# Two activation buffers of a TensorE-bound kernel laid out with 64 bytes between their chunks

## The reference

```
for i in range(2):                                   # first_block
    z = rmsnorm(x, g_mix) @ w_in                     # 2048 -> 4928
    y = concat(mla attention, gated short conv, gated 31-tap conv + layernorm, retention)
    x = x + y @ w_o                                  # 2048 -> 2048
    uf = causal_dwconv(rmsnorm(x, g_ffn) @ w_up)     # 2048 -> 11264, 3 taps
    x = x + (silu(gate) * up) @ w_down               # 5632 -> 2048
    x = x + (p @ w_pe) * sigmoid(rmsnorm(x, g_pe) @ w_pg)
for l in range(2):                                   # second_block
    q, k, v, gates = split(rms_norm(x, norm_g) @ w_in_2)   # 2048 -> 7700
    mixed = concat(forgetting, differential, block and gated linear attention)
    x = x + mixed @ w_out_2
return rms_norm(x, final_norm_g)
```

## Time and profile before

| | |
|---|---|
| median of three runs | 3352.53 us |
| profiled execution, its own time | 3352.41 us |
| its span, first to last instruction | 3350.2 us |
| busy share TensorE matmul / weight load | 99% / 87% |
| busy share VectorE / ScalarE / GpSimd | 78% / 46% / 26% |
| mean granted TensorE clock | 0.998 |
| DMA | 605 MB, 181 GB/s over the span |

### The profile page before, as it was taken

How to read it: one execution, slowest core, us unless ns; L and a number is a source line. 1 busy time by engine, 2 the same in 40 slices (tenths; PEclk the granted TensorE clock), 3 DMA queues, 4 the chain that set the end, 5 groups by cost and what they waited for, 6 DMA issues and landing times. The chain is left out here.

```text
span 3350.2 us, 53769 instructions
## 1 busy us (share of the span) xinstructions
PE 3327.6 (99%) x20366; PEld 2929.1 (87%) x20366; DVE 2617.8 (78%) x3394; ACT 1531.6 (46%) x1642; POOL 864.2 (26%) x633
## 2 busy tenths in 40 slices
PE   9999999999999999999999999999999999999998
PEld 8989888888888989888888888888888888888897
DVE  8897788787786888887887787867867866678865
ACT  5644444343433556544443434335444444445443
POOL 0422432121122423414332121214432004150004
PEclk9999999999999999999999999999999999999999
DMA  6445555555555554455555555555544455544454
GB/s 241 148 163 176 189 188 189 178 202 177 206 174 189 203 182 165 151 176 187 190 188 178 198 180 199 180 190 200 193 164 153 167 173 189 180 164 151 167 185 151
DMA packets 90647, 605.21 MB, mean 181 GB/s; under 512 B 10192, under 2 KB 10352, under 8 KB 29296
## 3 DMA queue, kind: packets, MB, share of 16 engines
q1 hardware_dynamic: 89424, 599.83, 52.0%
q10 hardware_dynamic: 1056, 3.11, 0.2%
HBM read 600.80 MB, written 2.10 MB: 180 GB/s over the span
## 5 line engine op out<-in xcount | busy, mean ns | idle before, releaser
L642 PE MATMUL bank<-H,whi 128*128 128x512 f32 x6496 | 1574.3, 393 | 1.5 <-DVE z L1661 1.5
L1164 ACT ACTIVATE whi<-raw 128x2048 fp32r<-128x2048 f32 (+2 forms) x609 | 1093.6, 1796 | 1044.6 <-DMA raw<-in_slabs_down 259.8
L1630 DVE TENSOR_TENSOR wlo<-raw,whi 128x2048 fp32r<-128x2048 f32 (+2 forms) x609 | 1328.4, 2181 | 243.2 <-ACT whi L1164 233.1
L642 PEld LDWEIGHTS bank<-H,whi 128*128 128x128 f32 x6496 | 1188.7, 188 | 238.6 <-issue 5.9
L653 PEld LDWEIGHTS bank<-H,wlo 128*128 128x128 f32 x6624 | 849.1, 188 | 34.3
L653 PE MATMUL bank<-H,wlo 128*128 128x256 f32 x6624 | 871.1, 281 | 0.0
L511 POOL TENSOR_TENSOR sqtmp<-tmp 128x256 f32<-128x256 f32 x88 | 218.9, 2488 | 867.8 <-DVE tmp L2211 867.8
L642 PE MATMUL bank<-G,whi 128*128 128x512 f32 x1408 | 343.0, 391 | 0.0
L642 PEld LDWEIGHTS bank<-G,whi 128*128 128x128 f32 x1408 | 255.4, 188 | 48.0
L1564 ACT ACTIVATE G<-sqtmp 128x256 f32 (+1 forms) x88 | 36.8, 418 | 404.0 <-POOL sqtmp L511 404.0
L489 POOL TENSOR_TENSOR sqacc<-sqacc,sqtmp 128x256 f32<-128x256 f32 x119 | 199.4, 1676 | 9.4
(11 more groups left out here) (390 smaller groups left out, 2881.4 us busy)
## 6 DMA issues: line engine op xcount, KB each, us to landing
raw<-in_slabs_up SPq DMA_DIRECT2D x176, 1024.0 KB, 4.8
raw<-in_slabs_down SPq DMA_DIRECT2D x128, 704.0 KB, 4.0
raw<-in_slabs_wo SPq DMA_DIRECT2D x32, 1024.0 KB, 4.8
raw<-in_slabs_pg SPq DMA_DIRECT2D x32, 1024.0 KB, 4.9
raw<-in_slabs_gates SPq DMA_DIRECT2D x32, 1024.0 KB, 4.9
raw<-in_slabs_wout SPq DMA_DIRECT2D x32, 1024.0 KB, 4.8
raw<-in_slabs_sc SPq DMA_DIRECT2D x24, 1024.0 KB, 4.8
raw<-in_slabs_fox SPq DMA_DIRECT2D x24, 1024.0 KB, 4.9
```

The costliest lines, as they stand in the source:

```text
L642: pe.matmul(b[0:r.m, :], whi[:, n % RAW, w], r.src[:, k, :], start=at == 0, stop=False)
L1164: act.activation(whi[:, n % RAW, 0:w], raw[:, n % RAW, 0:w], ACT.Copy).then_inc(S("hi_ready"), 1)
L1630: dve.tensor_tensor(wlo[:, n % RAW, 0:w], raw[:, n % RAW, 0:w], whi[:, n % RAW, 0:w].bitcast(F32), ALU.subtract).then_inc(S("lo_ready"), 1)
```

## The change

Chunks of `H` and of `G` no longer lie end to end: each is followed by 16 unused columns (64 bytes), so that the chunk step is 2112 bytes or 33 pieces. Chunk 0 starts at an even piece, chunk 1 at an odd one, and so on in turn; the stream of a wide or narrow row then starts at the other kind of piece from one product to the next. The second group of `G` starts at an odd piece, and alternates too. `whi`, `wlo`, `raw`, `x`, `z`, `y`, `tmp` and `pT_hl` keep the kind of piece that they had; the three unused tensors are made smaller to make room, so these buffers move by some hundred bytes (`raw` by 768, `whi` by 640, `z` by 256). For alternation within every row the `wout` rows (but for the two that open them) now take their chunks in the order 0 to 15. Apart from this every engine has the same instructions in the same order with the same waits.

```
+SPACED = 2 * T + 16
...
-    H = sb("H", [P, DC, 2 * T], F32R)
-    sb("ahead_of_raw", [P, 80])
+    H_spaced = sb("H", [P, DC, SPACED], F32R)
+    H = [H_spaced[:, c, 0:2 * T] for c in range(DC)]
+    sb("ahead_of_raw", [P, 16])
...
-    sb("ahead_of_whi", [P, 48])
+    sb("ahead_of_whi", [P, 16])
...
-    sb("ahead_of_z", [P, 104])
+    sb("ahead_of_z", [P, 8])
...
-    G = ctx.enter_context(nc.sbuf_tensor("G", [P, 2, GC, 2 * T], F32R))
-    ctx.enter_context(nc.sbuf_tensor("rest_of_y", [P, 48 * T - 2 * GC * 2 * T], F32))
+    G = sb("G", [P, 2, GC, SPACED], F32R)
+    sb("rest_of_y", [P, 48 * T - 2 * GC * SPACED])
+
+    def g_chunk(g, pair):
+
+        if isinstance(pair, int):
+            return G[:, g % 2, pair, 0:2 * T]
+        return G[:, g % 2, bass.ds(pair, 1), 0:2 * T].rearrange("p a t -> p (a t)")
...
-            src = G[:, key[2] % 2]
+            src = [g_chunk(key[2], c) for c in range(GC)]
...
-                        k = at if order is None else order[at]
+                        k = at
...
-                            pe.matmul(b[0:r.m, :], whi[:, n % RAW, w], r.src[:, k, :], start=at == 0, stop=False)
+                            pe.matmul(b[0:r.m, :], whi[:, n % RAW, w], r.src[k], start=at == 0, stop=False)
...
-                        last = pe.matmul(b[0:r.m, 0:T], wlo[:, n % RAW, w], r.src[:, k, 0:T], start=False,
+                        last = pe.matmul(b[0:r.m, 0:T], wlo[:, n % RAW, w], r.src[k][:, 0:T], start=False,
...
-                    high, low = (r.src[:, k, o + t * P:o + (t + 1) * P] for o in (0, T))
+                    high, low = (r.src[k][:, o + t * P:o + (t + 1) * P] for o in (0, T))
...
-                act.activation(H[:, c, 0:T], x[:, c, :], ACT.Copy, scale=col(g, l, c)).then_inc(S("h_hi"), 1)
+                act.activation(H[c][:, 0:T], x[:, c, :], ACT.Copy, scale=col(g, l, c)).then_inc(S("h_hi"), 1)
...
-                dve.scalar_tensor_tensor(H[:, c, T:2 * T], x[:, c, :], col(g, l, c), H[:, c, 0:T].bitcast(F32),
+                dve.scalar_tensor_tensor(H[c][:, T:2 * T], x[:, c, :], col(g, l, c), H[c][:, 0:T].bitcast(F32),
```

More of the change, by code:

```diff
@@ L341, in _build @@
     runs, by, h_free = [], {}, {}
-    sources = {"qn": cq, "qr": cq, "kv": cq[:, 4:6, :]}
+    latent = [cq[:, c, :] for c in range(6)]
+    sources = {"qn": latent[0:4], "qr": latent[0:4], "kv": latent[4:6]}
     for key, _, _, kt, m, count, _, _ in slab_table():
@@ L345, in _build @@
         if key[0] == "down":
-            src = G[:, key[2] % 2]
+            src = [g_chunk(key[2], c) for c in range(GC)]
         elif key[0] == "pe":
-            src = pT_hl[:, key[1]]
+            src = [pT_hl[:, key[1], c, :] for c in range(2)]
         loop = key[0] in ("wo", "up", "down", "pg", "wout")
@@ L512, in activations @@
                 pool.wait_ge(S("g_hi"), base + pair + 1)
-                gg = G[:, g % 2, bass.ds(pair, 1), :].rearrange("p a t -> p (a t)")
+                gg = g_chunk(g, pair)
                 pool.tensor_tensor(gg[:, T:2 * T], act_f[:], gg[:, 0:T].bitcast(F32),
@@ L584, in high_first @@
                     w = slice(k * r.m, (k + 1) * r.m)
-                    pe.matmul(b[:, 0:T], whi[:, n % RAW, w], r.src[:, k, 0:T], start=k == chunks[0], stop=False,
+                    pe.matmul(b[:, 0:T], whi[:, n % RAW, w], r.src[k][:, 0:T], start=k == chunks[0], stop=False,
                               skip_group_check=True)
-                    pe.matmul(b[:, 0:T], wlo[:, n % RAW, w], r.src[:, k, 0:T], start=False, stop=k == chunks[-1],
+                    pe.matmul(b[:, 0:T], wlo[:, n % RAW, w], r.src[k][:, 0:T], start=False, stop=k == chunks[-1],
                               skip_group_check=True)
@@ L595, in high_first @@
                         pe.wait_ge(S("h_ready"), h_base + rank[k] + 1)
-                    last = pe.matmul(b[:, T:2 * T], whi[:, n % RAW, k * r.m:(k + 1) * r.m], r.src[:, k, T:2 * T],
+                    last = pe.matmul(b[:, T:2 * T], whi[:, n % RAW, k * r.m:(k + 1) * r.m], r.src[k][:, T:2 * T],
                                      start=k == chunks[0], stop=k == chunks[-1], skip_group_check=True)
@@ L641, in run @@
                         if both:
-                            pe.matmul(b[0:r.m, :], whi[:, n % RAW, w], r.src[:, k, :], start=at == 0, stop=False)
+                            pe.matmul(b[0:r.m, :], whi[:, n % RAW, w], r.src[k], start=at == 0, stop=False)
                         else:
-                            pe.matmul(b[0:r.m, 0:T], whi[:, n % RAW, w], r.src[:, k, 0:T], start=at == 0, stop=False)
-                            pe.matmul(b[0:r.m, 0:T], whi[:, n % RAW, w], r.src[:, k, T:2 * T], start=False, stop=False)
+                            pe.matmul(b[0:r.m, 0:T], whi[:, n % RAW, w], r.src[k][:, 0:T], start=at == 0, stop=False)
+                            pe.matmul(b[0:r.m, 0:T], whi[:, n % RAW, w], r.src[k][:, T:2 * T], start=False, stop=False)
                     if both and not opening and first == 0:
@@ L702, in both_units @@
                             w = slice(8 * P * k + P * (2 * p + o), 8 * P * k + P * (2 * p + o + 1))
-                            pe.matmul(dst, whi[:, n % RAW, w], r.src[:, k, 0:T], start=k == 0, stop=False,
+                            pe.matmul(dst, whi[:, n % RAW, w], r.src[k][:, 0:T], start=k == 0, stop=False,
                                       skip_group_check=True)
-                            pe.matmul(dst, whi[:, n % RAW, w], r.src[:, k, T:2 * T], start=False, stop=False,
+                            pe.matmul(dst, whi[:, n % RAW, w], r.src[k][:, T:2 * T], start=False, stop=False,
                                       skip_group_check=True)
-                            last = pe.matmul(dst, wlo[:, n % RAW, w], r.src[:, k, 0:T], start=False, stop=k == 1,
+                            last = pe.matmul(dst, wlo[:, n % RAW, w], r.src[k][:, 0:T], start=False, stop=k == 1,
                                              skip_group_check=True)
@@ L744, in pair_unit @@
                         w = slice(r.m * k + P * (2 * p + o), r.m * k + P * (2 * p + o + 1))
-                        pe.matmul(dst, whi[:, n % RAW, w], r.src[:, k, 0:T], start=k == 0, stop=False,
+                        pe.matmul(dst, whi[:, n % RAW, w], r.src[k][:, 0:T], start=k == 0, stop=False,
                                   skip_group_check=True)
-                        pe.matmul(dst, whi[:, n % RAW, w], r.src[:, k, T:2 * T], start=False, stop=False,
+                        pe.matmul(dst, whi[:, n % RAW, w], r.src[k][:, T:2 * T], start=False, stop=False,
                                   skip_group_check=True)
-                        last = pe.matmul(dst, wlo[:, n % RAW, w], r.src[:, k, 0:T], start=False, stop=k == r.kt - 1,
+                        last = pe.matmul(dst, wlo[:, n % RAW, w], r.src[k][:, 0:T], start=False, stop=k == r.kt - 1,
                                          skip_group_check=True)
@@ L1225, in h_hi @@
                     act.wait_ge(S(name), base + c + 1)
-                act.activation(H[:, c, 0:T], src(c), ACT.Copy).then_inc(S("h_hi"), 1)
+                act.activation(H[c][:, 0:T], src(c), ACT.Copy).then_inc(S("h_hi"), 1)
         def x_hi(g, l, name, base, lo=0, hi=DC, handed=None):
@@ L1337, in beside_first @@
                     act.wait_ge(S("h_free"), h_free["rg", l] + c // 4 + 1)
-                    act.activation(H[:, c, 0:T], y[:, c, :], ACT.Copy).then_inc(S("h_hi"), 1)
+                    act.activation(H[c][:, 0:T], y[:, c, :], ACT.Copy).then_inc(S("h_hi"), 1)
             if 13 <= s < 29:
@@ L1563, in _ @@
                             act.wait_ge(S("act_f32"), 1 + pair + 1)
-                            act.activation(G[:, g % 2, bass.ds(2 * i + j // 2, 1), 0:T].rearrange("p a t -> p (a t)"),
+                            act.activation(g_chunk(g, 2 * i + j // 2)[:, 0:T],
                                            act_f[:], ACT.Copy).then_inc(S("g_hi"), 1)
@@ L1696, in y_lo @@
                 dve.wait_ge(S("h_hi"), DC * cnt["h"] + k + 1)
-                dve.tensor_tensor(H[:, c, T:2 * T], y[:, c, :], H[:, c, 0:T].bitcast(F32),
+                dve.tensor_tensor(H[c][:, T:2 * T], y[:, c, :], H[c][:, 0:T].bitcast(F32),
                                   ALU.subtract).then_inc(S("h_ready"), 1)
```

## The result

The change made the kernel slower: 3375.12 us, median of six runs, against 3352.61 us; ratio 1.0072, 95% interval 1.0062 to 1.0082. Forecast were 3385 us, in a range of 3315 to 3422. The profiled execution took 3375.12 us, its span is 3372.9 us, 22.7 us more than before.

What follows compares the result with a forecast made beforehand. TensorE, 99% busy, was taken to bound the kernel through its products' paces. The profiled 3352.4 us plus 26.5 for wide and 6 for narrow products gave 3384.9, so 3385 us was predicted, range 3315 to 3422.

Steps and rivals of the forecast that it cites:

- What bounds the kernel: Whole kernel: TensorE, 99% busy, never lacks work, so an edit counts only by what it does to its products' paces.
- Wide products: 512-column products of H and G: rows run unsettled at 232.0 ns, the value slabs' pace; together +26.5 us.
- paces snap to whole pieces: TensorE rows: settled paces are whole numbers of 64-byte pieces, 6.67 ns each, so even or odd starts can matter.
- the cost of the moved buffers: All engines: only addresses and the wout order change, no engine's instructions and no DMA; cost 0.
- Narrow products: 256-column products of H and G: alternating streams against odd weights take 118.4 ns; +6 us.
- the high-first rows: Rows of lines 585, 587 and 596: 118.4 ns with weights alternating, 120.0 with like starts; nearest rows for the narrow forecast.
- Value slabs, other engines, order of the wout rows: 960 value-slab products, bounds -5 to +4 us, taken as 0; VectorE and other engines 0; wout order 0.
- Rival A: Start of each wide product: alternation lets products go sooner, at 33 pieces, 220.0 ns, 3290 us; chance 0.30.
- A's weak form: Wide rows settle at 226.7 ns at once, without the five opening products: 3339 us; within A's 0.30.
- Rival B: Nothing happens: the excess is set by the instruction, not by addresses; 3352 us, give or take 4; chance 0.13.
- The rule of the Trainium skill: TensorE's stream and weight load have independent read ports, so addresses wouldn't count and the time would stay at 3352 us.
- Rival C: VectorE's splits slow by over 15% and TensorE waits on wlo: some 3400 us; chance 0.03.

Runs made afterwards that it cites:

- e4: Kernel after, but chunks end to end and H and G starting 64 bytes later, so every stream starts odd: 3367.69 us.
- e10: Kernel after, chunks end to end; distances (64-byte pieces, stream start to weight tile, modulo 4) of whi, wlo: H 2, 3; G 1, 2: 3386.77 us.
- e1: Kernel after with chunks of H and G end to end again, all other buffers left where the change put them: 3360.72 us, ratio 1.0027.
- e5: Kernel after, chunks end to end, whi put back to distance 0 and wlo at 1, other buffers elsewhere than before: 3352.14 us.
- e9: Kernel after with H spaced by 64 bytes, starting at whi 0, wlo 3; G end to end at whi 2, wlo 1: 3374.95 us.
- e7: Kernel after, chunks end to end, whi at distance 0 and wlo at 3 for H and G: 3364.12 us.
- e11: Kernel after, chunks end to end; H has whi and wlo at distance 0, G both at 2: 3365.79 us.
- e13: Layout of the kernel before, but the last chunk of H lies two pieces on, that of each G group one: 3347.10 us, ratio 0.9986.

## Why the prediction was right, and where it was not

- *What bounds the kernel.* This was right. TensorE is 99% busy in both, no wait came, VectorE's durations stayed, and the wide products alone take 24.7 us more, a little over the whole loss of 22.7.
- *Wide products.* The size was right: 232.0 ns taken from the value slabs, 231.9 measured for H; +20.4 us for H against 21.1, +4.3 for G against 5.4 (the pace there is 2.54 to 2.56 us a row). That it came out is in part luck: rows that don't settle took from 229.7 to 233.4 ns by the layout (e4, e10), and the reason for picking the value slabs was wrong.
- *Why they are slower.* Here the working was wrong though the number held. The argument was that paces snap to whole pieces, but the commonest narrow pace, 117.5 to 117.9 ns, is 17.6 to 17.7 pieces and doesn't. I took the kind of piece, even or odd, for what the settled pace hangs on, and put the cost of the moved buffers at 0. e1 refutes that step: with all streams even, the moved whi (distance 2 in place of 0) takes the settled pace away. In the kernel after two things take the settled pace away, and each alone is enough for that: the moved whi (e1 against e5), and the spacing, which makes the distance run through all values (e9 against e7). The value slabs, from which the number was taken, settle in e11, with both streams at distance 0.
- *Narrow products.* Forecast +6 us from the high-first rows, measured -0.7. The term was mis-sized: with the distance running through all values a narrow product of H takes 117.7 ns, not 118.4, and before it takes 117.9 in the median of all full rows, not the 117.5 of the one row read. What the spacing costs shows only against e1: there the moves alone had made the narrow rows faster by 15.7 us, and the spacing took 15.0 of them back. So of the measured +22.5 us, 8 come with the moves and some 14 with the spacing, and the 14 are in the narrow rows, while the prediction looked for the spacing's cost in the wide ones.
- *Value slabs, other engines, order of the wout rows.* These cost 0 each, as forecast: -0.3 us for the value slabs, and e5, with the straight order of the wout rows, has the time of before.
- *The range.* Rival A in its strong form (33 pieces, 220 ns) did not appear in any layout; the fastest has wide rows at 227.1 ns. In the argument against A, the unsettled pace of 232.0 ns lies 1.3 ns under 35 pieces and not 1.7. A's weak form, rows that are settled from the first product, is real (e13), but comes from one displaced chunk and not from alternation. Rival B is refuted by every layout with whi off distance 0: the pace depends on how stream and weights lie to each other, by up to 5 ns in 228. The rule of the Trainium skill ("SBUF — State Buffer", section "Who interferes with whom") that TensorE's two read ports are independent would have left the time as it was, and the measurement goes against that; whether the ports are where the two meet is not shown. Rival C did not occur.

**Open.** Why the period is 256 bytes, and which of the two, the product's own weights or the next one's, the stream meets: tiles of 8 pieces give both the same distance. Weight tiles spaced by 64 bytes, to step along with the chunks, were not run, so it is not shown that they would bring the settled pace back under spaced chunks. Why in e1 some narrow rows of H run at 113.9 ns and others at 117.9, and whether a settled wide row can be had together with fast narrow ones (by the paces some 35 us), is open too.

## What to carry to other kernels

Where TensorE is busy throughout, the pace of its products, start to start, is a number to watch on its own: take it from rows of one kind, and look whether it is constant within the row. If it depends on the layout, vary one distance between stream and weights at a time with everything else held, since a pad that is put in for one buffer moves all those behind it; the control that only moves is the first run to make, and here it would have shown that the theory of the change was not what it seemed. A right number from a neighbouring row (the value slabs) doesn't confirm the reason given for it.

## What the runs showed of the hardware

- fp32r products of 128x128 weights and 512 columns run at 226.7 ns in the settled state where stream and weight tile start at the same place modulo 256 bytes, and at 229.7 to 233.4 ns on the mean of a row elsewhere; products of 256 columns at 117.3 to 117.9, or 113.3 to 114.3, or up to 120.0 ns. With end-to-end chunks the narrow paces go by the distance of wlo the other way round: the row means are 119.3 and 119.6 ns at distance 0 (e4 G, e11 H), 118.4 to 118.6 at 2 (e4, e10, e11), and 117.6 to 117.9 or some 114 at 1 and 3. The granted clock was 0.997 to 0.999 in all.
- The pace of a row depends on how it is entered: the same 16 products took 3.65, 3.69 or 3.64 us (before, e7, e13) by what the row ahead and its last chunk did.
- VectorE's 2048-column subtraction takes 2323 to 2331 ns whether its two inputs start on like or unlike pieces.
